# Second-kind layers of an fp32 transformer kernel: convolution taps in two sums, GELU in one piece, keys ahead of values, no identity products, layer norm scaled on VectorE

## The reference

```python
h = rms_norm(x, norm_g);  z = h @ w_in            # then split by columns
# a: causal attention of 4 heads with a forget bias ("item 0")
o_a = fox_attention(fq, fk, fv, ff + fox_b) * silu(f_gate)
# b: gated depthwise convolution of 31 taps over 256 channels
y  = a * sigmoid(b);  y = conv31(y, conv_w) + conv_b
yn = (y - mu) * rsqrt(var + EPS) * ln_g + ln_b
o_b = (silu(yn) @ conv_pw) * silu(c_gate)
# c: 8 heads, 2 key groups; compressed, selected and window attention
def compress(x, pe, w1, w2):                      # 15 blocks of 32 tokens
    return gelu((blocks(x) + pe) @ w1) @ w2
k_cmp = rope(compress(kc, pe_k, k_w1, k_w2));  v_cmp = compress(vc, pe_v, v_w1, v_w2)
o_cmp = softmax(mask(q @ k_cmp)) @ v_cmp          # and o_slc, o_win: items 1 to 4
x = x + concat(o_a, o_b, (gated sum of o_cmp, o_slc, o_win) * silu(n_gate)) @ w_out
```

## Time and profile before

| what | value |
|---|---|
| runs of the kernel (3) | 1638.83, 1639.23, 1640.28 us |
| their median | 1639.23 us |
| the profiled execution, time | 1639.53 us |
| the profiled execution, span from first to last instruction | 1637.6 us |
| busy share of PE, DVE, ACT, POOL | 97%, 65%, 50%, 16% |
| mean granted clock of PE | 0.998 of full |
| third layer (first of the second kind) | some 1300 to 1465 us |
| fourth layer (second of the second kind) | some 1465 to 1630 us |

### The profile page before, as it was taken

The page is one execution under the profiler, slowest core; times in us unless marked ns, Lnnn a source line. Parts: engine busy times, 40 slices in busy tenths (PEclk is TensorE's granted clock), DMA queues, the critical chain, the costliest instruction groups (busy, mean ns, idle before and its releaser), DMA issues.

```text
span 1637.6 us, 27284 instructions
## 1 busy us (share of the span) xinstructions
PE 1591.2 (97%) x11240; PEld 1441.4 (88%) x11240; DVE 1066.5 (65%) x1269; ACT 825.7 (50%) x1123; POOL 258.3 (16%) x208
## 2 busy tenths in 40 slices
PE   7999999999999999999999999999999999999997
PEld 7999888888989999999988888898999898869885
DVE  4655558665755555655565867576555589968995
ACT  5443546653454343544454665345343475656563
POOL 0000060010000000000035001000000059405930
PEclk9999999999999999999999999999999999999999
DMA  7657555333455656555745434354655465046512
GB/s 228 228 184 236 180 176 173 123 129 101 159 180 185 201 183 202 169 193 193 236 155 188 156 118 134 104 190 146 210 189 195 132 211 201 33 136 216 196 33 90
DMA packets 206612, 273.97 MB, mean 167 GB/s; under 512 B 18774, under 2 KB 167096, under 8 KB 206008
## 3 DMA queue, kind: packets, MB, share of 16 engines
q1 hardware_dynamic: 206376, 272.67, 50.7%
q10 hardware_dynamic: 144, 0.00, 0.0%
HBM read 271.61 MB, written 1.08 MB: 167 GB/s over the span
## 4 chain that ended last, share of the span: by engine, by line
PE 83%; DVE 11%; ACT 3%; issue 2%; POOL 0%; DMA 0%; SPq 0%; POOLq 0%; ACTq 0%; DVEq 0%
PE bank L506 28%; PE bank L555 14%; PE bank L991 8%; PE bank L980 7%; PE bank L1181 4%; PE bank L2043 3%; DVE wlo L438 3%; PE bank L2299 2%; PE bank L1263 2%; PE bank L2021 2%; PE bank L1124 1%; DVE hT_lo L357 1%; PE bank L1099 1%; ACT whi L427 1%; PE bank L2196 1%
## 5 line engine op out<-in xcount | busy, mean ns | idle before, releaser
L438 DVE TENSOR_TENSOR wlo<-raw,whi 128x2048 fp32r<-128x2048 f32 (+2 forms) x258 | 584.6, 2269 | 325.7 <-ACT whi L427 324.9
L427 ACT ACTIVATE whi<-raw 128x2048 fp32r<-128x2048 f32 (+2 forms) x258 | 484.6, 1881 | 300.1 <-PE bank L555 102.0
L506 PE MATMUL bank<-hT_hi,whi 128*128 128x256 f32 x1408 | 393.0, 279 | 1.2 <-DVE wlo L438 0.5
L506 PE MATMUL bank<-hT_lo,whi 128*128 128x256 f32 x1408 | 390.0, 277 | 0.0
L506 PE MATMUL bank<-hT_hi,wlo 128*128 128x256 f32 x1408 | 389.9, 277 | 0.0
L506 PEld LDWEIGHTS bank<-hT_hi,whi 128*128 128x128 f32 x1408 | 264.9, 188 | 2.8 <-DVE wlo L438 1.6
L506 PEld LDWEIGHTS bank<-hT_lo,whi 128*128 128x128 f32 x1408 | 265.5, 189 | 0.0
L506 PEld LDWEIGHTS bank<-hT_hi,wlo 128*128 128x128 f32 x1408 | 264.7, 188 | 0.0
L555 PE MATMUL bank<-whi,Y 128*128 128x512 f32 (+5 forms) x748 | 224.8, 378 | 0.0
L555 PEld LDWEIGHTS bank<-whi,Y 128*128 128x128 f32 x748 | 140.3, 188 | 27.9
L311 POOL TENSOR_TENSOR st<-st 128x1 f32<-128x1 f32 x18 | 17.6, 979 | 926.7 <-ACT X L304 926.7
(11 more groups left out here) (398 smaller groups left out, 2829.9 us busy)
## 6 DMA issues: line engine op xcount, KB each, us to landing
raw<-in_ffn_w SPq DMA_DIRECT2D x132, 1024.0 KB, 5.3
raw<-in_w_in SPq DMA_DIRECT2D x80, 1024.0 KB, 5.4
raw<-in_w_out SPq DMA_DIRECT2D x16, 1024.0 KB, 4.8
raw<-in_w_br_na SPq DMA_DIRECT2D x4, 1024.0 KB, 5.4
raw<-in_w_br_mla SPq DMA_DIRECT2D x4, 1024.0 KB, 5.0
raw<-in_w_br_gla SPq DMA_DIRECT2D x4, 1024.0 KB, 5.0
raw<-in_cmp_k_w SPq DMA_DIRECT2D x4, 1024.0 KB, 5.7
raw<-in_cmp_v_w SPq DMA_DIRECT2D x4, 1024.0 KB, 5.3
```

What stands on the lines that cost most here:

```text
L427: act.activation(m["whi"][:, slot, 0:w], m["raw"][:, slot, 0:w], ACT.Copy).then_inc(s.hi_ready, 1)
L438: dve.tensor_tensor(m["wlo"][:, slot, 0:w], m["raw"][:, slot, 0:w], m["whi"][:, slot, 0:w].bitcast(F32), ALU.subtract).then_inc(s.lo_ready, 1)
L506: mm = pe.matmul(B[bank][:, mt * T:(mt + 1) * T], a, b, start=(n == 0 and k == 0), stop=(n == KK - 1 and k == 2))
```

## The change

Five edits, all in the layers of the second kind; the first kind, the helpers and the transfers stay as they are.

1. `taps` on DVE keeps two sums, one for even and one for odd taps, and waits only for the last but one tap. Tap 1 is a plain scaling; behind tap 30 one addition joins the sums.
2. `gelu` works on keys and values together (32x512 in place of twice 32x256) on DVE and ACT.
3. `cmp_kv` on DVE copies and rotates the keys first and copies the values behind that; the two memsets it began with are a step of their own, `cmp_zero`, ahead of `taps.0`. On PE the transpose of the keys is a step of its own, `cmp_kt`, and `heads_turn` and `cmp_kt` stand ahead of `value.0`.
4. `idle_products` is gone.
5. `ln.1` on DVE scales the squares and adds EPS while it copies them; POOL has only the power.

The three lists are reordered around these. Beside what follows from 1 to 4, `peak.0-2`, `exp.0-2` and `prob.0` stand earlier, and on ACT `tall.5` and `hi.17` stand later.

```diff
@@ Chain @@
     def __call__(self, ins):
+        self.until(self.step(ins))
+
+    def step(self, ins):
         self.n += 1
         ins.then_inc(self.sem, 1)
-        self.eng.wait_ge(self.sem, self.n)
+        return self.n
+
+    def until(self, n):
+        self.eng.wait_ge(self.sem, n)
@@ PE2 @@
-    tok_b.0 turn.0 tall.5 turn.1 hid_turn turn.2 cmp_kv value.0 heads_turn cmp_score scores.1 tall.6 scores.2 cmp_turn
+    tok_b.0 turn.0 tall.5 turn.1 hid_turn turn.2 cmp_kv heads_turn cmp_kt value.0 cmp_score scores.1 tall.6 scores.2 cmp_turn
@@ ACT2 @@
-    sq.1 hh.0-15 hi.2 params hi.3 sm hi.4 decay hi.5 fox_own tall.4 hi.6 tall.0 hi.7 blk.0-1 hi.8 tall.1-2 hi.9-12 exp.0 fv
-    hi.13-14 exp.1 hi.15-16 exp.2 tok_b.1 gelu.0 tok_b.0 turn.0 gelu.1 turn.1 tall.5 hid_turn turn.2 hi.17 heads_turn hi.18
+    sq.1 hh.0-15 hi.2 params hi.3 sm hi.4 decay hi.5 fox_own tall.4 hi.6 tall.0 hi.7 blk.0-1 hi.8 tall.1-2 hi.9-10 exp.0-2
+    hi.11-12 fv hi.13-16 tok_b.1 tok_b.0 gelu turn.0-1 hid_turn turn.2 tall.5 heads_turn hi.17 hi.18
@@ DVE2 @@
-    taps.0 lo.9 taps.1 peak.0 taps.2-3 lo.10-12 taps.4-5 sg lo.13 peak.1 taps.6 lo.14 peak.2 taps.7 lo.15 gelu.0 prob.0 gelu_out.0
-    gelu.1 lo.16 gelu_out.1 rotate cmp_kv tall.5 cmp_score lo.17 cmp_shift peak.3 taps.8-9 peak.4-5 cmp_prob tall.6 prob.1
+    cmp_zero taps.0 lo.9 peak.0-2 taps.1-2 lo.10 prob.0 lo.11-12 taps.3-4 sg lo.13 taps.5 lo.14 taps.6 lo.15 gelu lo.16 gelu_out
+    rotate cmp_kv cmp_score tall.5 lo.17 cmp_shift peak.3 taps.7-9 peak.4-5 cmp_prob tall.6 prob.1
@@ PE @@
-        def idle_products(n):
-
-            for _ in range(n):
-                pe.matmul(B[0][:, 0:P], ident, ident, start=True, stop=True)
-
-        def cmp_score():
-
-            idle_products(6)
+        def cmp_kt():
+
             pe.wait_ge(s.kcmp_ready, past.kcmp_ready + 1)
             pe.transpose(B[6][:, 128:192], kc2, ident[0:64, 0:64]).then_inc(s.kcmpT_done, 1)
-            idle_products(4)
+
+        def cmp_score():
+
             pe.wait_ge(s.vcmp_ready, past.vcmp_ready + 2)
@@ DVE @@
+        tap_done = [0, 0]
+
         def taps(k):
 
-            acc = cacc[:, 1, :]
+            sums = cacc[:, 1, :], cacc_odd
             for j in range(2 * k, min(2 * (k + 1), TAPS)):
-                src, w = padded[:, 1, j:j + T], conv_p[:, 1, j:j + 1]
+                acc, src, w = sums[j % 2], padded[:, 1, j:j + T], conv_p[:, 1, j:j + 1]
...
+                elif j == 1:
+                    ins = dve.tensor_scalar(acc, src, w, None, ALU.mult)
                 else:
-                    STT(acc, src, w, acc, ALU.mult, ALU.add).then_inc(s.conv_ready, 1)
+                    chain.until(tap_done[j % 2])
+                    ins = STT(acc, src, w, acc, ALU.mult, ALU.add)
+                tap_done[j % 2] = chain.step(ins)
+            if j == TAPS - 1:
+                chain.until(max(tap_done))
+                TTo(sums[0], sums[0], sums[1], ALU.add).then_inc(s.conv_ready, 1)
...
-        def cmp_kv():
+        def cmp_zero():
             chain(dve.memset(kc2, 0.0))
             chain(dve.memset(kcT, 0.0))
+
+        def cmp_kv():
             dve.wait_ge(s.cmp_done, past.cmp_done + 1)
+            rows = [slice(32 * g, 32 * g + N_CMP) for g in range(2)]
             for g in range(2):
-                rows = slice(32 * g, 32 * g + N_CMP)
-                dve.tensor_copy(kc2[rows, 0:64], B[7][rows, 0:64])
-                for odd in range(2):
-                    ins = dve.tensor_copy(vc[32 * odd:32 * odd + N_CMP, g], B[7][rows, 64:128])
-            ins.then_inc(s.vcmp_ready, 1)
-            dve.wait_ge(s.vcmp_ready, past.vcmp_ready + 1)
+                ins = dve.tensor_copy(kc2[rows[g], 0:64], B[7][rows[g], 0:64])
+            chain(ins)
             chain(rotate(kc2[:, 0:64].rearrange("p (t h n) -> p t h n", t=1, h=1), 1,
                          C("cos_cmp")[0:64, :], C("sin_cmp")[0:64, :]))
             dve.tensor_copy(kc2[:, 64:128], kc2[:, 0:64]).then_inc(s.kcmp_ready, 1)
+            for g in range(2):
+                for odd in range(2):
+                    ins = dve.tensor_copy(vc[32 * odd:32 * odd + N_CMP, g], B[7][rows[g], 64:128])
+            ins.then_inc(s.vcmp_ready, 1)
...
-                dve.tensor_copy(st[:, 40:42], B[6][:, 0:2]).then_inc(s.ln_var, 1)
+                dve.tensor_scalar(st[:, 40:42], B[6][:, 0:2], 1.0 / CONV_CH, EPS, ALU.mult, ALU.add).then_inc(s.ln_var, 1)
@@ POOL @@
         pool.wait_ge(s.ln_var, past.ln_var + 1)
-        chain(pool.tensor_scalar(st[:, 40:42], st[:, 40:42], 1.0 / CONV_CH, EPS, ALU.mult, ALU.add))
         pool.tensor_tensor(st[:, 42:44], st[:, 40:42], st[:, 255:256].to_broadcast([P, 2]), ALU.pow)\
             .then_inc(s.ln_rs, 1)
```

More of the change, by code:

```diff
@@ L2309, in _ @@
                  "w1": w1, "hid_turn": lambda i: hid_turn(), "cmp_kv": lambda i: cmp_kv(),
-                 "cmp_score": lambda i: cmp_score(), "cmp_turn": lambda i: cmp_turn(), "ln": ln,
+                 "cmp_kt": lambda i: cmp_kt(), "cmp_score": lambda i: cmp_score(), "cmp_turn": lambda i: cmp_turn(), "ln": ln,
                  "pw": lambda i: pw(), "wo": w_out}
@@ L2433, in out, with gelu @@
             act.activation(Y[:, tile:tile + 2, 0, :], yf.rearrange("p (i q) -> p i q", i=2), ACT.Copy).then_inc(s.yhi_ready, 1)
-        def gelu(v):
-            act.wait_ge(s.gelu_in, past.gelu_in + v + 1)
-            act.activation(gl_t[:, v, :], gl_t[:, v, :], ACT.Tanh, scale=float(np.sqrt(2 / np.pi))).then_inc(s.gelu_tanh, 1)
+        def gelu():
+            act.wait_ge(s.gelu_in, past.gelu_in + 1)
+            act.activation(gl_t, gl_t, ACT.Tanh, scale=float(np.sqrt(2 / np.pi))).then_inc(s.gelu_tanh, 1)
         def hid_turn():
@@ L2477, in _ @@
                  "params": lambda i: params(), "decay": lambda i: decay_step(), "fox_own": lambda i: fox_own(), "blk": block_high,
-                 "heads_turn": lambda i: heads_turn(), "exp": exp, "turn": turn, "out": out, "gelu": gelu,
+                 "heads_turn": lambda i: heads_turn(), "exp": exp, "turn": turn, "out": out, "gelu": lambda i: gelu(),
                  "hid_turn": lambda i: hid_turn(), "cmp_prob": lambda i: cmp_prob(), "cmp_turn": lambda i: cmp_turn(),
@@ L2594, in taps @@
                     dve.wait_ge(s.par_ready, past.par_ready + 1)
-                    chain(dve.tensor_scalar(acc, src, w, conv_p[:, 1, TAPS:TAPS + 1], ALU.mult, ALU.add))
-                elif j < TAPS - 1:
-                    chain(STT(acc, src, w, acc, ALU.mult, ALU.add))
-                else:
-                    STT(acc, src, w, acc, ALU.mult, ALU.add).then_inc(s.conv_ready, 1)
+                    ins = dve.tensor_scalar(acc, src, w, conv_p[:, 1, TAPS:TAPS + 1], ALU.mult, ALU.add)
+                elif j == 1:
+                    ins = dve.tensor_scalar(acc, src, w, None, ALU.mult)
+                else:
+                    chain.until(tap_done[j % 2])
[4 more added lines that the diff above has]
+                TTo(sums[0], sums[0], sums[1], ALU.add).then_inc(s.conv_ready, 1)
         def peak(j):
@@ L2750, in _ @@
                  "rotate": lambda i: rotary(), "taps": taps, "peak": peak, "prob": prob, "out": out, "out_low": out_low,
-                 "gelu": gelu, "gelu_out": gelu_out, "cmp_kv": lambda i: cmp_kv(), "cmp_score": lambda i: cmp_score(),
+                 "gelu": lambda i: gelu(), "gelu_out": lambda i: gelu_out(), "cmp_zero": lambda i: cmp_zero(), "cmp_kv": lambda i: cmp_kv(), "cmp_score": lambda i: cmp_score(),
                  "cmp_shift": lambda i: cmp_shift(), "cmp_prob": lambda i: cmp_prob(),
```

27 lines of the change are left out of this document (13 added, 14 removed).

## The result

The changed kernel takes **1643.4 us** (median of 20 runs, 1642.1 to 1646.2) against 1639.2 for the kernel before (20 runs): ratio 1.0024, 95% interval 1.0018 to 1.0030. It is slower by 4.2 us, outside my range (up to 1641.0) and on the side to which I gave 0.13. The profiled execution took 1643.95 us with a span of 1642.2; its mean granted TensorE clock was 0.993 (before 0.998). Over all 20 runs of the changed kernel that mean was 0.9925; over the 70 runs of the kernel before that were made beside the experiments it was 0.9969.

The account below looks back on a forecast made before the run. PE, busy in 97% of the span, was taken as the bound. Third layer -0.8 and fourth -1.4 make -2.2 us; +1.4 for one clock fall gives -0.8: 1638.5 us, range 1635.2 to 1641.0.

Parts of the forecast that it names:

- The wait of turn.0: PE's wait before turn.0 for DVE's softmax scaling goes: 0.52 us in the third layer, 1.5 in the fourth.
- P: The end of tall.5 on PE, from which later starts are counted; predicted 0.52 us earlier (third layer) and 1.5 (fourth).
- six taps before peak.4: On DVE before peak.4, six taps in place of four: 2.9 us, 0.4 later (ends 0.0 and 1.1).
- the holes: PE's idle stretch before scores.2 in each of the last two layers, waiting for ACT's exp.5: some 3.7 us.
- eleven taps at 0.12 less: DVE's taps behind scores.2, less a closing sum and its wait: 0.5 to 1 us; PE's waits of 0.56 and 0.16 go.
- one fall: The clock falls from 2.4 to 1.2 GHz before scores.2 in one layer of two, costing 1.4 us.
- the twenty passes: Unread identity products in PE's cmp_score, 3.22 us with a transpose and a wait, taken as only covering a wait.
- The hole that doesn't form: Rival, before scores.2: DVE's chain shortens as much as PE's, up to 3.7 us more a layer, 1629.7 us; chance 0.07.
- the power that isn't held: Rival, layer norm: DVE's lo.19 doesn't hold POOL's power, 1.1 us more gained a layer, 1636.3 us; chance 0.08.
- the two sums that bring nothing: Rival, DVE's taps: they stay at 0.52 us each, 1640.6 us; chance 0.12.
- the path that doesn't move: Rival: nothing on PE's path moves, 1639.2 us; chance 0.05.
- The slower rival: Both idle stretches before scores.2 lose the clock and it stays low into tall.7, 1649.5 us; chance 0.13.

Follow-up runs that it names:

- e1_fill: The changed kernel with fifteen unread products of the identity ahead of scores.2 on PE in both last layers: 1637.3 us, ratio 0.9990 to the kernel before.
- e9: The changed kernel with hi.17 between turn.0 and turn.1 on ACT, six identity products ahead of scores.2, and the taps in one sum again: 1637.4 us.
- e3_before_nofill: The kernel before without its twenty identity passes in cmp_score: 1644.7 us, ratio 1.0033 to the kernel before.

## Why the prediction was wrong, point by point

**Right.** The wait of turn.0 went in both layers. cmp_kv started at P+1.47 (predicted P+1.47), cmp_score at P+5.91 (5.9), PE stood before scores.2 at P+15.83 (15.8), lo.17 started at P+8.76 (8.75), DVE idled 2.18 us before it (2.3). Four undisturbed taps are 0.40 apart. From tall.7 to ln.2 the kernel takes 25.92 us in the fourth layer in place of 26.35, the 0.43 of the sum (0.16 + 0.27), and e1_fill has 25.92 in the third in place of 26.86 (0.94, predicted 0.83). The power took 2.71 us, the wait before ln.2 is 1.09. The rule that I took from the Trainium skill (VectorE: DVE Perf Modes, The DRAIN you can't avoid), that the next operation waits for an empty pipe and a semaphore costs nothing on top, would have kept the taps 0.5 apart. Those 0.40 disagree with it, and so does e9. The same section says that a next operation that isn't held starts earlier, which I left out.

**A term that was mis-sized: six taps before peak.4.** I took 2.9 us, "6 times 0.40 plus 0.5", where 0.5 was what four taps had lost beside POOL. They took 3.77. So scores.2 came 1.10 later after lo.17 than before (11.37 against 10.27), the end of my range (1.1) and not its middle (0.4), and the holes were 4.3 and 4.4, not 3.7. That POOL's own taps cause it is argued from the timelines alone (0.39 to 0.40 without them, 0.67 on average beside them); no run moved them away. It is 0.7 us a layer, 1.4 together. Another sum was off without weight: eleven taps at 0.12 less, against 0.4 and 0.5, give DVE 0.4, not "0.5 to 1".

**The step that failed: the clock.** "I take one fall, 1.4." Both holes lost the clock, and the low stretches cost 1.62 and 2.32 us, 3.94 in place of 1.4. One fall of two was a compromise that the rows didn't bear out: the same hole stands in both layers, and I had myself put it above the 2.3 us after which the earlier trace rows shows the fall. For these two holes the Trainium skill's warning of idle gaps (TensorE: Matmul & The Clock Gate, Why this matters for your kernels) was the better guide: both lost the clock, and e1_fill, which filled them, didn't. My price too came from the wrong rows: it let the low clock cover scores.2 (2.4 us of work), while it also covered cmp_turn and a part of the wait.

**What I never asked.** Taking out the twenty passes was entered as free, since nobody reads them. e3_before_nofill shows 5 us for them in the kernel before, where PE would have waited 1.6 and 1.2 us. These 5 us are no part of the 4.2: in the changed kernel value.0 stands in that place, PE waits at most 0.34 us there, and the clock is full there in both layers.

Nor did I look for a fall inside the run. The trace of the kernel before has one, behind a wait of only 1.68 us at the start of the third layer (first line: total, times and longest up to 1380; second: length, busy PE, PEld, DVE, ACT, POOL, clock, DMA share, GB/s):

```profile
PE bank L2069 <- DVE hT_lo L357: 1.9, 2, 1.7
...
1306.00:1308.00 2.00, 2.00 (x11) 2.00 (x11) 1.32 (x5) 1.54 (x5) 0.00 (x0) 0.50 0.00 0
```

So a fall can follow an idle stretch shorter than the 2.3 us of the earlier trace rows, and these are no threshold.

**The sum.** -2.2 predicted without the clock, +1.4 for the taps, +3.9 for the clock is +3.1; measured +4.2. The remaining 1.1 us go with falls at the starts of the layers (6.8 and 3.4 us low in the profile of after, 3.4 once in that of before). In the profiles, P comes 0.29 us earlier and not 0.52, and from the third layer's ln.2 to the fourth's cmp_kv the change wins 0.85 us (117.39 to 116.54) and not 1.98 (1.5 + 0.48). The change doesn't touch those starts, and why its profile has more falls there wasn't settled.

**The rivals.** The hole that doesn't form, the power that isn't held, the two sums that bring nothing and the path that doesn't move did not occur. The slower rival had the right mechanism and too much of it: both holes lost the clock, but it was back at 1410.6 and 1577.8, before tall.7, and tall.7 took 5.76 and 5.57 us (5.57 and 5.57 before). With the chance it got, 0.13, I let "it must last into tall.7" decide, though the forecast with both falls at their measured price, 1638.5 - 1.4 + 3.9 = 1641.0, already stands at the top of my range.

## What to carry to other kernels

Work on PE that nobody reads may hold its clock (e1, e3): before taking it out, list the waits that will be bare, and price each as its idle time plus, if the clock falls there, half of the low stretch in which PE has work (here 1.6 us for 3.4 and 2.3 us for 5.1), in every layer where it stands. When a chain is reordered so that one engine arrives early, look for what the order pushed back on the others: here a conversion behind a copy that comes late (hi.17) cost 2 to 3 us a layer, and one word moved in a list turned a loss of 4.2 us into a gain of 4.5. And read a small edit's worth from the distances in its own place too, not from the median alone: the two sums won 1.4 us there beside a hole of 4 us and 2.5 without it, while the medians said nothing and 5.0, because falls of the clock elsewhere came and went.
